# Softmax attention on pairs of heads, with the position bias reversed ahead of it, and a later slot for one subtraction after each norm

## The chip, the cores and the metric

The kernel runs on one core of a Trainium2 chip. Its time is the device time of one execution in microseconds (us). The core has TensorE (PE; its weight loads are listed as PEld), VectorE (DVE), ScalarE (ACT), GpSimd (POOL) and SyncE (SP), which issues DMAs. TensorE writes its results to PSUM, eight banks of 128 x 512 fp32; everything else works from SBUF. Each engine executes its instructions in the order in which they are written, and waits on semaphores for the others.

## The reference

The program is a stack of three blocks on 512 tokens of width 1024, all in fp32: two layers of `first_block`, then `second_block`. Each layer of the first has two gated feed-forwards, a mixer and a gated projection, with a norm after each; the mixer joins a gated delta rule, a stick-breaking attention and this one:

```python
def mla_attention(q_nope, q_rope, k_nope, k_rope, v):      # 4 heads, 96 values of q and k, 64 of v
    s = (einsum(qn, k_nope) + einsum(qr, k_rope)) * scale
    s = where(kpos <= qpos, s, -inf)                       # causal
    pr = softmax(s); return einsum(pr, v)
```

The mixer of the second block joins a sparse attention and a linear recurrence:

```python
def dsa_attention(q, k, v, q_idx, k_idx, w_idx, rel_bias): # 8 heads of 64
    score = sum over index heads of relu(q_idx . k_idx) * w_idx
    top_idx = top_k(score, 128)                            # the keys a query may see
    logits = q . k * HEAD_DIM ** -0.5 + rel_bias[t5_bucket(key - query)]
    p = softmax(logits over those keys); return p @ v

def rg_lru_branch(xr, gate, ...):
    r, i = sigmoid(xg @ w_a + b_a), sigmoid(xg @ w_i + b_i)
    a = exp(-8 * r * softplus(-lam)); b = sqrt(1 - a * a) * i * xc
    h = associative_scan(a, b); return h * gelu(gate)
```

## The kernel before

Activations stand transposed, features on partitions and the 512 tokens (`S`) along the row; a chunk is 128 features by 512 tokens. Weights come in blocks of 128 output features. Each block is loaded by SP, rounded by ScalarE (L171) and its remainder taken by VectorE (L178), and each product is three matmuls of rounded parts (L192 to L194). The program is a chain of stages; at the end of each all engines meet (`stage`, L121). The order on each engine is the order of the code.

`attention` (L1894) serves both softmax attentions. A unit is one head h and one block t of 128 queries, of w = (t + 1) * 128 keys, so the four units of a head have 128, 256, 384 and 512 columns. For a unit TensorE computes scores into one of four PSUM banks, VectorE masks them into SBUF (L2013 and L2014 in the first attention, L2429 in the second) and takes the maximum (L2015, L2430) and its negative (L1966), ScalarE takes exponentials with their sum (L1989), VectorE inverts the sum (L1952), GpSimd multiplies (L2000), TensorE transposes the weights block by block three units later (L1921), and VectorE copies them to SBUF (L1958). When the four units of a head are in, `weigh` (L1930) multiplies them with the values, four matmuls of 512, 384, 256 and 128 columns. ScalarE takes out each pair of heads (L1983). In the trace the first attention is `mix_ma`, the second `b_att`, the heads' outputs `heads_out`.

The bias of the second attention depends on key minus query. A DMA (L2457), in the stage `recurrence` before it (`b_rec`), lays out each head's row with a shift of one per partition, which gives it with the queries upside down; for every unit a matmul with the constant `flip` turns it over and adds it to the scores (L2424), ahead of the product of queries and keys (L2425). An fp32 matmul shows as two records of PE, a transpose as one. A head's queries and keys take 64 partitions, even heads the lower half, odd heads the upper.

In `recurrence` ScalarE evaluates two sigmoids, then per chunk two exponentials and a hyperbolic tangent (L2483 to L2485), then the roots (L2488), which need another table; VectorE then runs per chunk a product, a scan and the product with the gate (L2513 to L2515).

`NormHalves` ends each norm of the first block inside the stage that follows. VectorE multiplies x with the inverse deviation (L318) and subtracts the shift (L323), for parts of 1, 1, 2, 2 and 2 chunks; ScalarE applies gain and bias (L302) and rounds (L305); VectorE takes the remainder, `low` (L311), in the places that the loop at L315 gives. `multiply_first` lets TensorE begin with the chunks that are ready. The stages are the mixer's projections (`mix_proj`), the second feed-forward (`ffb`) and the gated projection (`ple`), each in two layers.

Of the kernel before, what the change touches and what calls it, by code (L numbers as in the profile page):

```python
# [20 lines left out]
F32 = mybir.dt.float32  # L21
# [6 lines left out]
P = 128  # L28
# [251 lines left out]
class NormHalves:  # L280
# [27 lines left out]
    def vector(self, dve, x_high, x_low, beside=nothing):  # L308
# [7 lines left out]
        for part, (begin, end) in enumerate(self.PARTS):  # L316
# [7 lines left out]
            if part > 0:  # L324
                low(n_low)
                n_low += 1
# [1564 lines left out]
RING = 4  # L1891


def attention(nc, name, heads, scores, masked, values, out, scale, const, preload=False):  # L1894
# [5 lines left out]
    units = [(h, t) for h in range(heads) for t in range(NT)]  # L1900
    dims = 64
    with ExitStack() as ctx:
        sb = lambda n, s: ctx.enter_context(nc.sbuf_tensor(f"{name}_{n}", s, F32))
        bank = lambda n: ctx.enter_context(nc.psum_tensor(f"{name}_{n}", [P, S], F32))
        sc, p, pt = sb("sc", [P, 2, S]), sb("p", [P, RING, S]), sb("pt", [P, 2, NT, S])
        stat = sb("stat", [P, RING, 4])
        ps, pr, po = ([bank(f"{n}{j}") for j in range(k)] for n, k in (("s", RING), ("t", 2), ("o", 2)))
        with stage(nc, name, ["scored", "dve_step", "max_ready", "exp_ready", "inverted", "normed", "turned",
                              "pt_ready", "o_done", "o_taken"]) as (
                block, scored, dve_step, max_ready, exp_ready, inverted, normed, turned,  # L1910
                pt_ready, o_done, o_taken):

            @block.tensor
            def _(pe):
                def turn(n):

                    h, t = units[n]
                    pe.wait_ge(normed, n + 1)
                    at_least(pe, pt_ready, n - 1)
                    for s in range(t + 1):  # L1920
                        mm = pe.transpose(pr[n % 2][:, s * P:(s + 1) * P], p[:, n % RING, s * P:(s + 1) * P], const["ident"])  # L1921
                    mm.then_inc(turned, 1)

                def weigh(h):
                    rows = slice(h % 2 * dims, (h % 2 + 1) * dims)
                    pe.wait_ge(pt_ready, NT * (h + 1))
                    if h % 2 == 0:
                        at_least(pe, o_taken, h // 2 - 1)
                    for s in range(NT):
                        mm = pe.matmul(po[h // 2 % 2][rows, s * P:], values(h, s), pt[:, h % 2, s, s * P:],  # L1930
                                       start=s == 0, stop=s == NT - 1, skip_group_check=True)
# [900 lines left out]
```

## Time and profile before

| | us |
|---|---|
| three runs, median (lowest to highest) | 3978.52 (3978.36 to 3985.76) |
| the profiled execution, its own time | 3990.3 |
| its span in the profile | 3988.5 |
| TensorE busy in the span | 3628.1 |
| mean granted clock of TensorE | 0.95 of full speed |

The rows below are lines of one profiled execution. Times are us from the start of the span unless marked ns. A line of a timeline has its start, its length, the engine, the source line, the operation, output<-inputs, the shape, and in brackets the idle time before it and who ended it. A line of windows has the stretch and its length, then busy us with the number of instructions for PE, PEld, DVE, ACT and POOL, then the granted clock of TensorE (1.00 is 2.4 GHz, 0.50 is 1.2 GHz), the share of DMA and GB/s. The end of a matmul is modelled and matmuls overlap, so the distance between starts is its cost. The profile shortens `b2_` to `b_`.

### The profile page before, as it was taken

How to read it: one execution, taken by the hardware profiler on the slowest of the kernel's cores; microseconds unless marked ns; L12 is line 12 of the kernel's file. 1: busy time of each engine (PE TensorE's matmuls, PEld its weight loads, DVE VectorE, ACT ScalarE, POOL GpSimd, SP SyncE). 2: the span in 40 equal slices, each digit the busy share in tenths (PEclk: the TensorE clock that was granted, in tenths of full speed). 3: DMA queues.
4: the chain of work that ended last, by engine and by line, in shares of the span. 5: the costliest groups of instructions: out<-in, count | busy, mean ns of one | idle time of the engine just before them, and what ended most of it. 6: DMA issues, size and time to landing. Idle time of an engine off the chain costs nothing. (4 is left out here: it accounts for less than half of the span.)

```text
span 3988.5 us, 47143 instructions
## 1 busy us (share of the span) xinstructions
PE 3628.1 (91%) x19474; PEld 2768.7 (69%) x19474; DVE 1779.6 (45%) x2352; ACT 1198.9 (30%) x1683; POOL 520.2 (13%) x466
## 2 busy tenths in 40 slices
PE   7999897898999799989979899987999797869997
PEld 5888664676887578867638577865888575347886
DVE  5542365445642455333555455333332365643322
ACT  2222333233222322233332422224222324223221
POOL 0002012430002000020134200021000200330001
PEclk9999999899999899999989899998999898879998
DMA  4432110013331233312100133312333122012231
GB/s 153 142 120 87 63 59 28 2 44 111 135 119 64 90 132 138 107 62 74 65 1 4 59 136 137 105 59 70 93 94 107 52 79 69 1 53 82 94 106 58
DMA packets 88133, 324.23 MB, mean 81 GB/s; under 512 B 12648, under 2 KB 14696, under 8 KB 87536
## 3 DMA queue, kind: packets, MB, share of 16 engines
q1 hardware_dynamic: 87920, 321.21, 24.0%
q8 instruction: 155, 2.54, 0.3%
q14 instruction: 58, 0.48, 0.0%
HBM read 319.06 MB, written 2.12 MB: 81 GB/s over the span
## 5 line engine op out<-in xcount | busy, mean ns | idle before, releaser
L178 DVE TENSOR_TENSOR w_low<-w_raw,w_high 128x1024 fp32r<-128x1024 f32 (+2 forms) x496 | 636.8, 1285 | 1269.8 <-ACT w_high L171 1269.0
L171 ACT ACTIVATE w_high<-w_raw 128x1024 fp32r<-128x1024 f32 (+2 forms) x496 | 544.7, 1099 | 1436.9 <-PE ffa_ps L194 455.5
L192 PE MATMUL ffa_ps<-ffa_x_high,w_high 128*128 128x512 f32 x704 | 283.1, 402 | 34.9 <-DVE ffa_x_low L238 31.3
L192 PE MATMUL ffb_ps<-ffb_x_high,w_high 128*128 128x512 f32 x704 | 285.6, 406 | 27.4 <-DVE ffb_x_low L311 21.4
L192 PE MATMUL b_f_ps<-b_f_x_high,w_high 128*128 128x512 f32 x704 | 281.6, 400 | 18.7 <-DVE b_f_x_low L359 15.1
L193 PE MATMUL ffb_ps<-ffb_x_low,w_high 128*128 128x512 f32 x704 | 283.0, 402 | 0.0
L193 PE MATMUL ffa_ps<-ffa_x_low,w_high 128*128 128x512 f32 x704 | 281.5, 400 | 0.0
L194 PE MATMUL ffb_ps<-ffb_x_high,w_low 128*128 128x512 f32 x704 | 281.4, 400 | 0.0
L194 PE MATMUL ffa_ps<-ffa_x_high,w_low 128*128 128x512 f32 x704 | 281.1, 399 | 0.0
L193 PE MATMUL b_f_ps<-b_f_x_low,w_high 128*128 128x512 f32 x704 | 280.3, 398 | 0.0
L194 PE MATMUL b_f_ps<-b_f_x_high,w_low 128*128 128x512 f32 x704 | 280.1, 398 | 0.0
L192 PE MATMUL mix_proj_ps<-mix_x_high,w_high 128*128 128x512 f32 x432 | 178.4, 413 | 25.8 <-DVE mix_x_low L311 22.4
L192 PEld LDWEIGHTS ffa_ps<-ffa_x_high,w_high 128*128 128x128 f32 x704 | 134.1, 190 | 67.4 <-DVE w_low L178 36.1
L192 PEld LDWEIGHTS ffb_ps<-ffb_x_high,w_high 128*128 128x128 f32 x704 | 134.5, 191 | 66.6 <-issue 24.0
L192 PEld LDWEIGHTS b_f_ps<-b_f_x_high,w_high 128*128 128x128 f32 x704 | 134.1, 190 | 56.1 <-issue 16.9
L193 PE MATMUL mix_proj_ps<-mix_x_low,w_high 128*128 128x512 f32 x432 | 172.3, 399 | 0.0
L194 PE MATMUL mix_proj_ps<-mix_x_high,w_low 128*128 128x512 f32 x432 | 172.2, 398 | 0.0
L194 PEld LDWEIGHTS ffb_ps<-ffb_x_high,w_low 128*128 128x128 f32 x704 | 134.5, 191 | 32.0
L194 PEld LDWEIGHTS b_f_ps<-b_f_x_high,w_low 128*128 128x128 f32 x704 | 134.2, 191 | 31.7
L194 PEld LDWEIGHTS ffa_ps<-ffa_x_high,w_low 128*128 128x128 f32 x704 | 133.9, 190 | 31.6
L193 PEld LDWEIGHTS ffa_ps<-ffa_x_low,w_high 128*128 128x128 f32 x704 | 134.0, 190 | 31.4
L193 PEld LDWEIGHTS ffb_ps<-ffb_x_low,w_high 128*128 128x128 f32 x704 | 134.7, 191 | 30.2
(519 smaller groups left out, 6863.2 us busy)
## 6 DMA issues: line engine op xcount, KB each, us to landing
w_raw<-in_ffa_in SPq DMA_DIRECT2D x88, 512.0 KB, 3.3
w_raw<-in_ffb_in SPq DMA_DIRECT2D x88, 512.0 KB, 3.3
w_raw<-in_ffn_in SPq DMA_DIRECT2D x88, 512.0 KB, 3.5
w_raw<-in_mix_in SPq DMA_DIRECT2D x80, 512.0 KB, 3.4
w_raw<-in_ffa_out SPq DMA_DIRECT2D x32, 704.0 KB, 4.0
w_raw<-in_ffb_out SPq DMA_DIRECT2D x32, 704.0 KB, 4.0
w_raw<-in_ffn_out SPq DMA_DIRECT2D x32, 704.0 KB, 4.0
ffa_ada_raw<-in_w_ada SPq DMA_DIRECT2D x36, 512.0 KB, 4.2
```

The costliest lines, as they stand in the source:

```text
L171: act.activation(self.high[:, n % HALVES, :cols], self.raw[:, n % SLOTS, :cols], ACT.Copy).then_inc(self.rounded, 1)
L178: dve.tensor_tensor(self.low[:, n % HALVES, :cols], self.raw[:, n % SLOTS, :cols], self.high[:, n % HALVES, :cols].bitcast(F32), ALU.subtr ...
L192: pe.matmul(out, w_high, x_high[:, k0 + k, :], start=start and k == 0, stop=False)
L193: pe.matmul(out, w_high, x_low[:, k0 + k, :], start=False, stop=False)
L194: mm = pe.matmul(out, w_low, x_high[:, k0 + k, :], start=False, stop=stop and k == kt - 1)
```

## The change

A unit becomes a pair of heads g and one block t of queries; the buffers have a third index a for the head of the pair. There are two score tiles of two banks each, two banks `pr` for transposes (one for each head of the pair) and two for outputs. TensorE scores both heads of unit n when the exponentials of unit n - 2 are done, transposes unit n - 3 and weighs unit n - 4 block by block, with matmuls of 128 columns that alternate between the two heads. VectorE masks, reduces and scales for both heads in one instruction each; in the first attention the mask is added in place in PSUM, to the last 128 columns alone, and ScalarE reads the scores from PSUM. ScalarE copies the transposed weights in place of VectorE. GpSimd's multiplication is a tensor_tensor over both heads with the inverse repeated. In the second attention GpSimd also adds bias and selection mask into `added`, one unit ahead, and VectorE adds that to the scores. The bias is turned over in `recurrence`, by eight matmuls of 512 columns after the gates and eight copies on ScalarE after the tanh of the last chunk. In `NormHalves` the second `low` of a part is taken only for a chunk of an earlier part.

```diff
-            if part > 0:
+            if n_low < begin:
                 low(n_low)
                 n_low += 1
...
-                for n, (h, t) in enumerate(units):
-                    at_least(pe, max_ready, n - RING + 1)
-                    scores(pe, h, t, ps[n % RING]).then_inc(scored, 1)
-                    if n >= RING - 1:
-                        turn(n - RING + 1)
-                    if t == NT - 1 and h:
-                        weigh(h - 1)
...
+                def turn(n):
+                    g, t = units[n]
+                    pe.wait_ge(normed, n + 1)
+                    for a in range(2):
+                        at_least(pe, pt_ready, 2 * (n - 1) + a + 1)
+                        for s in range(t + 1):
+                            mm = pe.transpose(pr[a][:, s * P:(s + 1) * P], p[:, n % ring, a, s * P:(s + 1) * P], const["ident"])
+                        mm.then_inc(turned, 1)
+                def weigh(n):
+                    g, t = units[n]
+                    pe.wait_ge(pt_ready, 2 * (n + 1))
...
+                    for s in range(t + 1):
+                        for a in range(2):
+                            mm = pe.matmul(po[g % 2][a * dims:(a + 1) * dims, t * P:(t + 1) * P], values(2 * g + a, s),
+                                           pt[:, n % 2, a, s * P:(s + 1) * P], start=s == 0, stop=s == t, skip_group_check=True)
+                for n in range(count + ring):
+                    if n < count:
+                        at_least(pe, exp_ready, 2 * (n - 1))
+                        for a in range(2):
+                            mm = scores(pe, *units[n], a, ps[n % 2])
+                        mm.then_inc(scored, 1)
+                    if 0 <= n - ring + 1 < count:
+                        turn(n - ring + 1)
+                    if n >= ring:
+                        weigh(n - ring)
...
+                        source = masked(dve, own, units[n][1], ps[n % 2], p[:, slot, :, :], added and added[:, n % 2, :, 0:w])
+                        own(dve.tensor_reduce(top[:, slot, :], source, AX_X, ALU.max))
+                        dve.tensor_scalar(shift[:, slot, :], top[:, slot, :], -scale, None, ALU.mult).then_inc(max_ready, 1)
+                    if n:
+                        dve.wait_ge(exp_ready, 2 * n)
+                        dve.reciprocal(inverse[:, (n - 1) % ring, :], total[:, (n - 1) % ring, :]).then_inc(inverted, 1)
...
+                        for a in range(2):
+                            source = p[:, slot, a, 0:w] if bias else ps[n % 2][:, a, 0:w]
+                            act.activation(p[:, slot, a, 0:w], source, ACT.Exp, bias=shift[:, slot, a:a + 1], scale=scale,
+                                           accum_out=total[:, slot, a:a + 1]).then_inc(exp_ready, 1)
+                    if n >= ring - 1:
+                        take(n - ring + 1)
...
+                    if bias and n + 1 < count:
+                        add(n + 1)
+                    pool.wait_ge(inverted, n + 1)
+                    pool.tensor_tensor(p[:, slot, :, 0:w], p[:, slot, :, 0:w], repeat(inverse[:, slot, :], 2, w), ALU.mult)\
                         .then_inc(normed, 1)
...
 def sparse_attention(nc, name, m, const):
-        pe.matmul(ps[:, 0:w], const["flip"], m.bias[:, h, S - w:S], start=True, stop=False)
-        return pe.matmul(ps[:, 0:w], m.q[rows, h // 2, t * P:w], m.k[rows, h // 2, 0:w], start=False, stop=True)
+        return pe.matmul(ps[:, a, 0:w], m.q[rows, g, t * P:w], m.k[rows, g, 0:w], start=True, stop=True)
+    def bias(pool, dst, g, t):
+        return pool.tensor_tensor(dst, m.bias[:, 2 * g:2 * g + 2, S - w:S], repeat(m.drop[:, t, 0:w], 1, 2), ALU.add)
+        own(dve.tensor_tensor(p[:, :, 0:w], ps[:, :, 0:w], added, ALU.add))
...
 def recurrence(nc, name, m, rows_dram, const):
+                pe.wait_ge(bias_landed, 16)
+                for h in range(AH):
+                    at_least(pe, bias_ready, h - 3)
+                    pe.matmul(flipped[h % 4][:, :], const["flip"], m.bias[:, h, :], start=True, stop=True).then_inc(bias_flipped, 1)
...
+                for h in range(AH):
+                    act.wait_ge(bias_flipped, h + 1)
+                    act.activation(m.bias[:, h, :], flipped[h % 4][:, :], ACT.Copy).then_inc(bias_ready, 1)
                 for c in range(LC):
                     act.wait_ge(variance, c + 1)
                     act.activation(a2[:, c, :], a2[:, c, :], ACT.Sqrt).then_inc(rooted, 1)
```

TensorE in the second attention before, from the second head's third block on (`b_att_s` scores, `b_att_t` transposed weights, `b_att_o` outputs, `squares` the constants):

```order
L2424 MATMUL b_att_s<-b_bias,squares 128x384
L2425 MATMUL b_att_s<-b_k,b_q 128x384
L1921 MATMUL b_att_t<-squares,b_att_p 128x128 x4
L2424 MATMUL b_att_s<-b_bias,squares 128x512
L2425 MATMUL b_att_s<-b_k,b_q 128x512
L1921 MATMUL b_att_t<-squares,b_att_p 128x128
L1930 MATMUL b_att_o<-b_att_pt,b_v 64x512
L1930 MATMUL b_att_o<-b_att_pt,b_v 64x384
L1930 MATMUL b_att_o<-b_att_pt,b_v 64x256
L1930 MATMUL b_att_o<-b_att_pt,b_v 64x128
```

The same engine and stage now, from the second pair's first block on:

```order
L2431 MATMUL b_att_s<-b_k,b_q 128x128 x2
L1922 MATMUL b_att_t<-squares,b_att_p 128x128 x4
L1932 MATMUL b_att_o<-b_att_pt,b_v 64x128 x2
L2431 MATMUL b_att_s<-b_k,b_q 128x256 x2
L1922 MATMUL b_att_t<-squares,b_att_p 128x128 x6
L1932 MATMUL b_att_o<-b_att_pt,b_v 64x128 x4
L2431 MATMUL b_att_s<-b_k,b_q 128x384 x2
L1922 MATMUL b_att_t<-squares,b_att_p 128x128 x8
L1932 MATMUL b_att_o<-b_att_pt,b_v 64x128 x6
```

The matmul with `flip` is gone, and each unit now ends with weighing in pieces of 128 columns.

ScalarE in the recurrence before, its last chunk (`b_rec_a`, `b_rec_th` the exponentials and the tanh):

```order
L2483 ACTIVATE b_rec_a<-b_rec_r,b_rec_slope 128x512
L2484 ACTIVATE b_rec_a<-b_rec_r,b_rec_twice 128x512
L2485 ACTIVATE b_rec_th<-b_rec_r,b_rec_minus 128x512
L2488 ACT_TABLE_LOAD
L2488 ACTIVATE b_rec_a<-b_rec_a 128x512 x4
```

And now (`b_rec_flip` the turned bias):

```order
L2497 ACTIVATE b_rec_a<-b_rec_r,b_rec_slope 128x512
L2498 ACTIVATE b_rec_a<-b_rec_r,b_rec_twice 128x512
L2499 ACTIVATE b_rec_th<-b_rec_r,b_rec_minus 128x512
L2502 ACTIVATE b_bias<-b_rec_flip 128x512 x8
L2505 ACT_TABLE_LOAD
L2505 ACTIVATE b_rec_a<-b_rec_a 128x512 x4
```

Eight copies stand between the last tanh and the roots' table load.

VectorE after the norm ahead of the mixer before, from the third part on:

```order
L318 TENSOR_TENSOR state<-state,norm 128x1024
L311 TENSOR_TENSOR mix_x_low<-state,mix_x_high 128x512
L323 TENSOR_TENSOR state<-state,norm 128x1024
L311 TENSOR_TENSOR mix_x_low<-state,mix_x_high 128x512
L318 TENSOR_TENSOR state<-state,norm 128x1024
L311 TENSOR_TENSOR mix_x_low<-state,mix_x_high 128x512
L323 TENSOR_TENSOR state<-state,norm 128x1024
L311 TENSOR_TENSOR mix_x_low<-state,mix_x_high 128x512
```

And now:

```order
L318 TENSOR_TENSOR state<-state,norm 128x1024
L311 TENSOR_TENSOR mix_x_low<-state,mix_x_high 128x512
L323 TENSOR_TENSOR state<-state,norm 128x1024
L318 TENSOR_TENSOR state<-state,norm 128x1024
L311 TENSOR_TENSOR mix_x_low<-state,mix_x_high 128x512
L323 TENSOR_TENSOR state<-state,norm 128x1024
L311 TENSOR_TENSOR mix_x_low<-state,mix_x_high 128x512
```

The next part's product now stands ahead of the `low` that waits for the part just finished.

## Rows read from the trace of the kernel before

**Rows 1.** The page, part 1: busy us, share of the span, instructions

```profile
PE 3628.1 (91%) x19474; PEld 2768.7 (69%) x19474; DVE 1779.6 (45%) x2352; ACT 1198.9 (30%) x1683; POOL 520.2 (13%) x466
```

**Rows 2.** Windows: first attention twice, recurrence, second attention; columns in the text above

```profile
656.80:694.30 37.50, 27.44 (x104) 14.26 (x104) 27.10 (x92) 11.55 (x34) 17.25 (x16) 0.91 0.00 1
2017.60:2055.90 38.30, 29.27 (x104) 15.30 (x104) 27.25 (x92) 11.54 (x34) 17.25 (x16) 0.87 0.00 1
3368.30:3400.60 32.30, 8.80 (x16) 3.54 (x16) 13.65 (x22) 21.42 (x31) 4.98 (x4) 0.62 0.20 65
3400.60:3490.70 90.10, 87.40 (x272) 39.43 (x272) 52.67 (x160) 24.26 (x69) 34.59 (x32) 0.85 0.00 1
```

**Rows 3.** Timeline of PE, second attention, clock full: start, duration, engine, line, tiles

```profile
3432.55 0.66 PE L1921 MATMUL b_att_t<-squares,b_att_p 128*128 128x128 f32 x4
...
3433.04 1.02 PE L2424 MATMUL b_att_s<-b_bias,squares 128*128 128x512 f32 x2
...
3433.99 1.12 PE L2425 MATMUL b_att_s<-b_k,b_q 64*128 64x512 f32 x2
...
3435.05 0.33 PE L1921 MATMUL b_att_t<-squares,b_att_p 128*128 128x128 f32 x1
...
3435.30 2.37 PE L1930 MATMUL b_att_o<-b_att_pt,b_v 128*64 128x512 f32 x8
```

**Rows 4.** Timeline of PE, first attention in layer 0: its first four scores

```profile
656.79 2.40 PE L2007 MATMUL mix_ma_s<-mix_km,mix_qm 96*128 96x128 f32 x8 [2.18 <-PEq L128]
```

**Rows 5.** Timeline of PE: key selection, 64-row matmuls in alternating halves

```profile
3290.68 3.42 PE L2255 MATMUL b_proj_keys_ps<-b_ki,b_qi 64*128 64x512 f32 x10
```

**Rows 6.** Groups of the second attention: count, busy us, mean ns, idle before

```profile
L1989 ACT ACTIVATE b_att_p<-b_att_sc,b_att_stat 128x128 f32<-128x128 f32 (+3 forms) x32 | 18.0, 562 | 59.8 <-DVE b_att_stat L1966 59.6
...
L2429 DVE TENSOR_TENSOR b_att_sc<-b_att_s,b_drop 128x128 f32<-128x128 f32 (+3 forms) x32 | 15.7, 491 | 30.7 <-PE b_att_s L2425 28.5 <-POOL b_att_p L2000 2.2
...
L1989 ACT ACTIVATION_READ_ACCUMULATOR b_att_p<-b_att_sc,b_att_stat 128x1 f32 x32 | 6.0, 186 | 0.0
...
L1983 ACT ACTIVATE b_heads_out<-b_att_o 128x512 f32<-128x512 f32 x4 | 2.3, 582 | 6.0 <-PE b_att_o L1930 6.0
```

**Rows 7.** Groups of GpSimd by shape, whole span

```profile
L1553 POOL TENSOR_TENSOR mix_gc_nb<-mix_gc_lt,squares 128x512 f32<-128x512 f32 x48 | 60.5, 1272 | 81.1 <-PE mix_gc_py L1366 50.1 <-DVE mix_gc_xt L1612 31.0
...
L604 POOL TENSOR_TENSOR ffa_sq_sum<-ffa_sq_sum,ffa_square 128x512 f32<-128x512 f32 x10 | 18.4, 1839 | 22.2 <-ACT ffa_square L618 21.9
...
L905 POOL TENSOR_TENSOR gdn<-gdn,squares 128x128 f32<-128x128 f32 x32 | 15.5, 483 | 5.6 <-ACT gdn L886 5.6
```

**Rows 8.** Windows: clock in the second attention's start, then in the first

```profile
3400.60:3424.00 23.40, 23.36 (x42) 9.70 (x42) 9.45 (x31) 5.70 (x15) 5.83 (x6) 0.50 0.00 1
...
3427.00:3430.00 3.00, 3.00 (x15) 1.70 (x13) 0.67 (x4) 0.00 (x0) 0.27 (x1) 0.91 0.00 0
664.00:668.00 4.00, 4.00 (x11) 2.60 (x12) 3.19 (x12) 0.85 (x3) 2.13 (x3) 0.50 0.00 0
```

**Rows 9.** Timeline of the recurrence: table load before the roots, first root's user

```profile
3386.77 1.28 ACT L2488 ACT_TABLE_LOAD   x1
...
3388.73 0.69 DVE L2513 TENSOR_TENSOR b_rec_th<-b_rec_a,b_rec_i 128x512 f32<-128x512 f32 x1 [1.25 <-ACT b_rec_a L2488]
```

**Rows 10.** Timelines: waits for x_low after norms, mix and ffb, both layers

```profile
433.68 0.47 PE L192 MATMUL mix_proj_ps<-mix_x_high,w_high 128*128 128x512 f32 x1 [1.28 <-DVE mix_x_low L311]
...
926.06 0.48 PE L192 MATMUL ffb_ps<-ffb_x_high,w_high 128*128 128x512 f32 x1 [1.68 <-DVE ffb_x_low L311]
...
1789.28 0.47 PE L192 MATMUL mix_proj_ps<-mix_x_high,w_high 128*128 128x512 f32 x1 [0.73 <-DVE mix_x_low L311]
...
1794.39 0.47 PE L192 MATMUL mix_proj_ps<-mix_x_high,w_high 128*128 128x512 f32 x1 [1.73 <-DVE mix_x_low L311]
...
1793.55 0.69 DVE L311 TENSOR_TENSOR mix_x_low<-state,mix_x_high 128x512 fp32r<-128x512 f32 x1 [1.54 <-ACT mix_x_high L305]
...
2288.57 0.48 PE L192 MATMUL ffb_ps<-ffb_x_high,w_high 128*128 128x512 f32 x1 [0.42 <-DVE ffb_x_low L311]
```

More of the change, by code:

```diff
@@ L1888, in _, with attention @@
                     turn(h + 1, m.qm[rope, h, :])
[L1891 to L1901, printed above, removed]
+def attention(nc, name, pairs, scores, masked, values, out, scale, const, preload=False, bias=None):
+    units = [(g, t) for g in range(pairs) for t in range(NT)]
+    dims, ring = 64, 4
     with ExitStack() as ctx:
[L1903 to L1908, printed above, removed]
+        sb = lambda n, *s: ctx.enter_context(nc.sbuf_tensor(f"{name}_{n}", [P, *s], F32))
+        bank = lambda n, *s: ctx.enter_context(nc.psum_tensor(f"{name}_{n}", [P, *s], F32))
+        p, pt = sb("p", ring, 2, S), sb("pt", 2, 2, S)
+        added = sb("added", 2, 2, S) if bias else None
+        top, shift, total, inverse = (sb(n, ring, 2) for n in ("top", "shift", "total", "inverse"))
+        ps = [bank(f"s{j}", 2, S) for j in range(2)]
+        pr, po = [bank(f"t{j}", S) for j in range(2)], [bank(f"o{j}", S) for j in range(2)]
+        with stage(nc, name, ["scored", "dve_step", "bias_ready", "max_ready", "exp_ready", "inverted", "normed", "turned",
                               "pt_ready", "o_done", "o_taken"]) as (
-                block, scored, dve_step, max_ready, exp_ready, inverted, normed, turned,
+                block, scored, dve_step, bias_ready, max_ready, exp_ready, inverted, normed, turned,
                 pt_ready, o_done, o_taken):
+            count = len(units)
             @block.tensor
@@ L1993, in _, with take, take_out @@
-                take_out(heads // 2 - 1)
+                def take(n):
+                    w = (units[n][1] + 1) * P
+                    for a in range(2):
+                        act.wait_ge(turned, 2 * n + a + 1)
+                        at_least(act, o_done, n - 1)
+                        act.activation(pt[:, n % 2, a, 0:w], pr[a][:, 0:w], ACT.Copy).then_inc(pt_ready, 1)
+                def take_out(g):
+                    act.wait_ge(o_done, NT * (g + 1))
+                    act.activation(out(g), po[g % 2][:, :], ACT.Copy).then_inc(o_taken, 1)
@@ L2009, in masked, with scores @@
[L2009 to L2018 removed]
+    def scores(pe, g, t, a, ps):
+        h, w = 2 * g + a, (t + 1) * P
+        return pe.matmul(ps[:, a, 0:w], m.qm[0:MQ, h, t * P:w], m.km[0:MQ, h, 0:w], start=True, stop=True)
@@ L2021, in first_mixer, with masked @@
+    def masked(dve, own, t, ps, p, added):
+        last = ps[:, :, t * P:(t + 1) * P]
+        own(dve.tensor_tensor(last, last, repeat(const["causal"], 1, 2), ALU.add))
+        return ps[:, :, 0:(t + 1) * P]
+    attention(nc, name, MH // 2, scores, masked, lambda h, s: m.vm[:, s, h * MV:(h + 1) * MV],
+              lambda g: m.o[:, GC + SBH // 2 + g, :], float(MQ) ** -0.5, const)
 def first_mixer(nc, ws, name, halves, m, const, dram):
```

115 lines of the change are left out of this document (40 added, 75 removed).

## Prediction, made before the changed kernel was run

> **What bounds the kernel now.** First the page: TensorE is busy for 3628 of 3988 us [rows 1], so only a place where it stalls, or works more than the output needs, can give time. Then one row of windows for each touched stage [rows 2]: the first attention takes 37.5 us in layer 0 and 38.3 in layer 1, the recurrence 32.3, the second attention 90.1. Within them TensorE is busy for 27.4, 29.3, 8.8 and 87.4. So the second attention is bound by TensorE, the first by the hand-over between engines, and the recurrence by ScalarE and then VectorE, with TensorE out of work. The clock comes next [rows 8]: for the first 23.4 us of the second attention it is 0.50 though TensorE is never idle, and it is back (0.91) only in 3427 to 3430; the first attention has such a spell too, at 664. The last view is the timeline around the norms' ends [rows 10].
>
> All terms below are against the profiled execution (3990.3 us, span 3988.5); the forecast moves the median of the three runs, 3978.5, by the same amount.
>
> **Prices.** At full clock, per pass: a score of 512 columns costs 0.95 us with 128 rows and 1.06 with 64 (3433.04 to 3433.99 to 3435.05) [rows 3], and four transposes 0.49, thus 0.12 each. A head's weighing is 2.37 us, of which some 0.17 is the tail of the last matmul. The four scores of a head with 96 rows are 2.40, or 2.23 without the tail [rows 4]. At half clock I double all of these.
>
> **Second attention.** (a) The bias's matmuls leave the stage: 0.95 us for 512 columns (3433.04 to 3433.99 [rows 3]), 1280 columns a head thus 2.4, eight heads 19 us at full clock, more in the part at half clock. (b) The scores of a pair now follow each other in alternating halves of the partitions. The trace has that form: ten records of 512 columns in 3.42 us [rows 5], 0.33 each against 0.53 for the lone one of rows 3. With 320 columns on average and four records, a unit costs 0.83 us; without overlap it is 1.32, the other bound. (c) On average a unit has five transposes (20 for a pair's four units): five by 0.12 is 0.6, I take 0.57. (d) Weighing in pieces of 128 columns: the multiplications are the same columns, two heads' 2.2 without the tail, 4.4 us a pair, so 1.1 a unit; the weight loads rise from 8 to 20 records a head and hide as those of the transposes do. If the two column halves overlap as the rows do, it is 0.55. I take 1.1. TensorE then needs 2.5 us a unit, 40 for sixteen.
>
> (e) VectorE: an instruction for 320 columns takes 0.49 [rows 6], for two heads 0.83 (twice, less one fixed part of 0.15). Addition, maximum and the small scaling come to 1.9. (f) ScalarE: two exponentials and their reads 1.4, two copies 0.85 (0.58 for 512 columns, less for fewer). (g) GpSimd: 0.48 us for 128 columns and 1.27 for 512 [rows 7] make 2.1 ns a column, so 0.74, 1.28, 1.81 and 2.34 for the four sizes of a pair, 6.2 for all; bias and normalising both need it, 12.3 a pair, 49 for the stage. The dearest row is 1.84 for 512 [rows 7], which makes 18.3 a pair and 73 for the stage. I take the first, the commonest (48 instructions).
>
> (h) The loop: with two score tiles, unit n's scores wait for the exponentials of n - 2, and stand on TensorE behind the transposes and weighing of iteration n - 1, which wait for ScalarE's copies of iteration n - 2. So two units need at least 2.5 + 1.9 + 1.4 + 0.85 and about 0.3 for five hand-overs, 6.95 us: 3.5 a unit, above TensorE's 2.5 and GpSimd's 3.1. Sixteen units make 56. At the end come the last unit's normalising 2.3, transposes 0.9, copies 1.1, weighing 0.9, output 0.6; the first three units have nothing to transpose or weigh, which gives 3 back: 59. (i) The clock: at half clock TensorE's part of two units' round is 2.5 us longer, which makes 4.7 instead of 3.5 a unit; a spell of 26 us as now would cost 6.6. I take nearly all of it, 6: **65, from 90.1: -25**.
>
> In the Trainium skill, "TensorEngine Tiling (Array Packing)", section "Key Properties", says that different tiles of the array can run at the same time, but also that changing the tiling mode drains TensorE. The trace agrees with the first half (0.33 against 0.53 a record). The second speaks against this change, which goes from half rows to the whole array to half columns in every unit; rows 3 put a change at about 0.1 us (1.06 less 0.95), so 48 changes would be 5 us in the stage if each lay in the loop. By that the stage would be 68.
>
> The Trainium skill, "GPSIMD Engine Reference", section "Specifications", puts GpSimd's contention with VectorE at instructions of VectorE with two SBUF inputs. Here VectorE's additions have one input in PSUM. By that rule GpSimd keeps the 1.27 [rows 7] and needs 49 us; by the row of 1.84 it is 73. No row of before has this pair of operations side by side.
>
> **First attention, twice.** TensorE: a pair has the scores of two heads, 2 x 2.23 over its four units, 1.12 a unit; with transposes 0.57 and weighing 1.1 it is 2.8. VectorE's mask is now 256 columns (0.42), the maximum 0.83: 1.5 with the scaling. ScalarE 1.4 + 0.85, hand-overs 0.3. Two units take 6.85, one 3.4, eight 27.4. With the end (5.8) and 2.5 back at the start it is 31. A half-clock spell of 7 us, as at 664, costs 2. So 33 against 37.5 and 38.3: **-9.8** together. Bounds: 29.5 with no spell (-17), and 46 with the clock at half throughout, where TensorE's 5.6 a unit is the bound (+16).
>
> **Recurrence.** TensorE's first four turned heads are ready before ScalarE ends the last tanh at 3386.8 and cost nothing; the cover is that TensorE is idle there. ScalarE makes four copies at 0.5, which frees banks one by one; TensorE, by then at half clock, needs 1.75 us (0.95 doubled, less a fixed part) for each of the last four from 3387.4 on, so the last copy ends near 3395. Only then come table load and first root: the product that waits for it, now at 3388.7 [rows 9], moves by **+8.2** (3395 less 3386.8). All of VectorE's chain behind it moves with it. Bounds: 4.9 with TensorE at full clock, 9 with later starts. The DMA of the bias (issued with the stage's start) has landed by then.
>
> **Norms' ends.** VectorE now does the next part's product (1024 columns, by the 0.69 of 512 some 1.25) in the 1.54 us for which it waits for ScalarE [rows 10]. From the fourth part on each `low` comes earlier, the last by about 3.3. The last waits of TensorE for it are 1.28, 1.68, 0.73 and 1.73, and 0.42 in layer 1's feed-forward [rows 10]: 5.8 us, all gone. In `ple` TensorE waits for weights that stand behind `low` on VectorE; I take 1 us for each layer, between 0 and 3.3. **-7.8**. What is late next is the third block's remainder, which waits for TensorE itself.
>
> **Sum.** -25 - 9.8 + 8.2 - 7.8 = -34.4: 3944 us.
>
> **The rivals.**
> - *GpSimd becomes the bound.* For it: with 3.1 us a unit it has more work than TensorE's 2.5 even at the lower price, and a row of 1.84 [rows 7] is the higher. Against: 48 instructions show the lower price, 10 the higher. The stage is 73 + 8 = 81, a gain of 9: the sum is -18.4, 3960.
> - *More overlap.* Column halves overlap too and the clock holds. The second attention is 57 and the first 29.5 each: -33 - 17 + 5 - 8 = -53, 3926. For it: rows 5. Against: the clock fell in both stages.
> - *Half clock for half of each stage.* The short 128-column work leaves TensorE waiting in the loop, 2.5 of 3.5 us busy. Attentions at 76 and 40 each: -14 + 4 = -10, and the rest cancels: 3969.
> - *Slower: half clock to the end in both attentions.* Then TensorE needs 5.0 to 5.6 us a unit and binds: 86 to 102 us in the second, 46 twice in the first (+16). With 86 that is -4 + 16 + 0.4 = +12, 3991; with 102 it is +28. It decides from the point where TensorE is slow for more than about two thirds of both stages. For it: rows 8, 23 us at 0.50 with TensorE never idle. Against: once up, the clock stayed up through the rest of both stages with TensorE 73% busy or less [rows 2], and it will be 71 to 82% busy.
> - *The change does not do what it says:* the bias's matmuls could return as waits. They are not in the stage any more, so only the clock and GpSimd can take the gain back; both are above.
>
> **How the numbers follow.** Forecast 57% (own range 3932 to 3956), more overlap 10%, GpSimd 15%, half clock for half of it 10%, slower 8%. The range to hold 8 of 10 is 3924 to 3968. A measurement can tell 0.2%, 8 us, from no change, not less. Faster by more than that: the first three and half of the fourth, 87%; within it 6%; slower 7%.
>
> **What would show it.** The second attention's window near 65 us with TensorE some 65% busy, and pairs of 512-column scores starting within 1.4 us; eight units of the first near 33; the first root's user near 20 us (now 20.4) + 8 from the recurrence's start; no wait of TensorE for `x_low` after its fourth chunk. GpSimd idle for under a tenth of the second attention would mean the first rival, a clock below 0.75 over the stages the third or fourth. The forecast is wrong if either attention's loop is longer than 4.2 us a unit, or if the recurrence grows by over 10.

## The result, and the profile after

The changed kernel takes 3956.15 us (median of four runs, 3955.25 to 3957.4) against 3982.14 (3978.36 to 3986.51) for the kernel before: a ratio of 0.9932, 95% interval 0.9918 to 0.9945, or 26 us less. Forecast were 34 less and 3944. The 3956 lies in the stated range, but 26 less is about as near to the rival in which GpSimd becomes the bound (18 less) as to the forecast, so the whole time alone does not choose between them. The profiled executions differ by 34 (spans 3988.5 and 3954.6), but that of before was 8 us over its median, so their agreement with the sum of the terms is an accident. The terms must be read one by one.

The page of the changed kernel, part 1, beside [rows 1]:

```profile
PE 3586.2 (91%) x19618; PEld 2761.9 (70%) x19618; DVE 1729.2 (44%) x2136; ACT 1221.4 (31%) x1755; POOL 515.1 (13%) x450
```

The touched stages, from barrier to barrier, in the order first attention twice, recurrence, second attention. First the kernel before (the windows of [rows 2], drawn out to the barriers), then the changed one:

```profile
656.60:695.20 38.60, 27.45 (x104) 14.30 (x104) 27.10 (x92) 11.55 (x34) 17.25 (x16) 0.91 0.00 1
2017.50:2056.40 38.90, 29.27 (x104) 15.30 (x104) 27.25 (x92) 11.54 (x34) 17.25 (x16) 0.87 0.00 1
...
3400.50:3492.30 91.80, 87.40 (x272) 39.43 (x272) 52.67 (x160) 24.26 (x69) 34.59 (x32) 0.85 0.00 1
```

```profile
652.50:687.70 35.20, 28.09 (x152) 18.09 (x152) 12.50 (x32) 15.97 (x50) 10.02 (x8) 0.76 0.01 1
2001.00:2036.00 35.00, 28.24 (x152) 18.27 (x152) 12.50 (x32) 15.97 (x50) 10.03 (x8) 0.76 0.00 1
3335.30:3375.30 40.00, 18.93 (x32) 7.56 (x32) 13.65 (x22) 25.73 (x39) 5.00 (x4) 0.69 0.15 53
3375.30:3460.80 85.50, 53.66 (x304) 32.22 (x304) 30.20 (x64) 33.39 (x101) 43.97 (x32) 0.65 0.00 1
```

The second attention's engines have far less to do (TensorE 53.7 us in place of 87.4), no engine is busy for more than 63% of it, and yet it is only 6.3 us shorter. That is where the expected gain went. Its timeline shows why. One steady stretch of the changed kernel, picked rows of GpSimd and VectorE:

```profile
3423.79 1.04 POOL L2011 TENSOR_TENSOR b_att_p<-b_att_p,b_att_inverse 128x512 f32<-128x512 f32 x1 [2.49 <-DVE b_att_inverse L1964]
...
3424.79 2.34 POOL L2435 TENSOR_TENSOR b_att_added<-b_bias,b_drop 128x1024 f32<-128x1024 f32 x1
...
3427.33 1.23 DVE L2439 TENSOR_TENSOR b_att_p<-b_att_s,b_att_added 128x1024 f32<-128x1024 f32 x1 [3.62 <-POOL b_att_added L2435]
...
3428.59 1.22 DVE L1960 TENSOR_REDUCE b_att_top<-b_att_p 128x2 f32<-128x1024 f32 x1
3429.85 0.17 DVE L1961 TENSOR_SCALAR b_att_shift<-b_att_top 128x2 f32<-128x2 f32 x1
3429.92 0.16 DVE L1964 RECIPROCAL b_att_inverse<-b_att_total 128x2 f32<-128x2 f32 x1
...
3430.16 1.47 POOL L2011 TENSOR_TENSOR b_att_p<-b_att_p,b_att_inverse 128x768 f32<-128x768 f32 x1 [3.03 <-DVE b_att_inverse L1964]
```

Read it as a ring, which is a closed loop of waits. GpSimd normalises unit n, then adds bias and mask for n + 2; VectorE waits for just that (3.62 us), then adds, reduces and scales n + 2, and only behind that inverts the sum of n + 1; GpSimd waits for just that (3.03) and normalises n + 1. The two take turns. A pair of heads, four units, takes 19.9 us (3418.91 to 3438.81). GpSimd's eight instructions (0.61, 1.81, 1.04, 2.34, 1.47, 0.72, 1.89, 1.26) are 11.1 of it, its four waits for the inverse (2.49, 3.03, 1.43, 1.96) the other 8.9. That is 4.98 a unit, 80 for the stage, and more than the 4.2 a unit that the prediction named as a sign of being wrong.

The groups of the same stage name it too, in their last column (the 29.2 ahead of the first is one wait, for the stage to begin):

```profile
L2435 POOL TENSOR_TENSOR b_att_added<-b_bias,b_drop 128x256 f32<-128x256 f32 (+3 forms) x16 | 24.5, 1535 | 29.2 <-SPq L125 29.2
L2011 POOL TENSOR_TENSOR b_att_p<-b_att_p,b_att_inverse 128x256 f32<-128x256 f32 (+3 forms) x16 | 20.0, 1252 | 34.2 <-DVE b_att_inverse L1964 34.2
...
L2439 DVE TENSOR_TENSOR b_att_p<-b_att_s,b_att_added 128x256 f32<-128x256 f32 (+3 forms) x16 | 13.2, 825 | 44.8 <-POOL b_att_added L2435 37.1 <-PE b_att_t L1922 5.3 <-PE b_att_s L2431 2.3
```

In the recurrence the table load ahead of the roots and the first root's user answer to [rows 9]:

```profile
3361.69 1.28 ACT L2505 ACT_TABLE_LOAD   x1
...
3363.64 0.69 DVE L2530 TENSOR_TENSOR b_rec_th<-b_rec_a,b_rec_i 128x512 f32<-128x512 f32 x1 [9.12 <-ACT b_rec_a L2505]
```

From the stage's start that user stands at 28.3 us, against 20.4. Of the waits for `x_low` in [rows 10] none is left in mix or ffb. The last one in layer 0's mixer is now this, for the third chunk, and the other three stages have one of the same length at the same place:

```profile
421.07 0.79 PE L192 MATMUL mix_proj_ps<-mix_x_high,w_high 128*128 128x512 f32 x1 [1.72 <-DVE mix_x_low L311]
```

### The profile page after: what moved, and what is told of

It reads as the page before. It is cut to its first block and busy times, and to the rows that moved or that the text cites. A ratio compares the mean times of both kernels' runs of the same rounds, so it can differ in the third digit from the quotient of the medians.

```text
span 3954.6 us, 47146 instructions
## 1 busy us (share of the span) xinstructions
PE 3586.2 (91%) x19618; PEld 2761.9 (70%) x19618; DVE 1729.2 (44%) x2136; ACT 1221.4 (31%) x1755; POOL 515.1 (13%) x450
## 5 line engine op out<-in xcount | busy, mean ns | idle before, releaser
L192 PE MATMUL ffa_ps<-ffa_x_high,w_high 128*128 128x512 f32 x704 | 281.7, 400 | 35.4 <-DVE ffa_x_low L238 31.8
L193 PEld LDWEIGHTS b_f_ps<-b_f_x_low,w_high 128*128 128x128 f32 x704 | 133.8, 190 | 30.7
L193 PEld LDWEIGHTS ffb_ps<-ffb_x_low,w_high 128*128 128x128 f32 x704 | 133.7, 190 | 30.6
```

The costliest lines, as they stand in the source:

```text
L192: pe.matmul(out, w_high, x_high[:, k0 + k, :], start=start and k == 0, stop=False)
L193: pe.matmul(out, w_high, x_low[:, k0 + k, :], start=False, stop=False)
```

## The experiments

The ratios are to the kernel before, run on the same chip between the others, with 95% intervals. Stages are from barrier to barrier in one profiled execution each. The same code differs there from run to run: the recurrence of the changed kernel has 40.1 us here and 38.5 in add_two_ahead, the first attention of before 38.6 and 38.9 here and 37.9 and 37.4 in norms_only.

| | ratio | first attention | recurrence | second attention |
|---|---|---|---|---|
| before | 1 | 38.6, 38.9 | 32.2 | 91.8 |
| norms_only | 0.9963 (0.9951 to 0.9976) | 37.9, 37.4 | 32.2 | 91.8 |
| changed kernel | 0.9932 (0.9918 to 0.9945) | 35.3, 35.0 | 40.1 | 85.5 |
| add_two_ahead | 0.9867 (0.9851 to 0.9884) | 35.2, 35.0 | 38.5 | 62.2 |
| inverse_first | 0.9906 (0.9889 to 0.9922) | 35.1, 35.0 | 38.9 | 74.5 |
| warm | 0.9941 (0.9927 to 0.9955) | 31.8, 35.0 | 40.1 | 85.5 |
| take_first | 0.9932 (0.9917 to 0.9947) | 29.8, 29.2 | 40.1 | 84.7 |
| roots_first | 0.9906 (0.9883 to 0.9928) | 35.1, 34.9 | 32.2 | 86.0 |
| by_head | one run, 3958.5 us | 32.6, 35.7 | 40.1 | 85.7 |
| add2_roots_take | 0.9834 (0.9816 to 0.9851) | 29.2, 30.6 | 32.2 | 57.2 |
| scale_on_act | 0.9821 (0.9805 to 0.9838) | 29.7, 30.6 | 32.2 | 55.2 |
| warm_start | 0.9835 (0.9817 to 0.9854) | 30.8, 29.4 | 32.2 | 57.3 |
| no_addition | one run, 3913.2 us | 27.1, 29.2 | 32.2 | 53.9 |

**norms_only.** The kernel before with the `NormHalves` part of the diff alone.

> The kernel before with one part of the change alone: after a norm the second low of a part is taken only for a chunk of an earlier part. The prediction's price is -7.8 us for all six places (5.8 in mix and ffb, 1 in each ple). In the profile of the changed kernel the stages mix_proj are 1.6 and 1.5 us shorter, ffb 3.2 and 6.6, ple 5.7 and 3.0, in all 21.6, part of it the clock (ffb of layer 1 has 0.4 us to win at its wait). Theory (waits alone): -6 to -10 us, a ratio of 0.9975 to 0.9985. Rival (the norms' ends bring most of the whole kernel's gain): -20 us, 0.995. Other rival (the gain is in the profile only): 0, 1.000.

Its stages give -1.6 and -1.6 us in mix_proj, -3.3 and -2.6 in ffb, -5.4 and -2.6 in ple: -17.1. The ratio gives -14.7 (-9.6 to -19.5). That is between the first theory and the rival, and about twice the forecast of 7.8. By the medians this part brings more than half of what the whole change does; the interval allows from a third to three quarters. Layer 0's ple, the kernel before and then this one:

```profile
1321.86 0.69 DVE L311 TENSOR_TENSOR ple_x_low<-state,ple_x_high 128x512 fp32r<-128x512 f32 x1 [1.54 <-ACT ple_x_high L305]
1322.94 0.51 PE L192 MATMUL ple_proj<-ple_p_high,w_high 128*128 128x512 f32 x1 [2.04 <-DVE w_low L178]
1325.82 0.50 PE L192 MATMUL ple_ps<-ple_x_high,w_high 128*128 128x512 f32 x1 [1.21 <-DVE w_low L178]
```

```profile
1314.76 0.69 DVE L311 TENSOR_TENSOR ple_x_low<-state,ple_x_high 128x512 fp32r<-128x512 f32 x1
1315.84 0.50 PE L192 MATMUL ple_proj<-ple_p_high,w_high 128*128 128x512 f32 x1 [0.41 <-DVE w_low L178]
1318.71 0.50 PE L192 MATMUL ple_ps<-ple_x_high,w_high 128*128 128x512 f32 x1 [1.21 <-DVE w_low L178]
```

VectorE's wait ahead of the `low` is gone, and TensorE's wait for the weights behind it is 0.41 in place of 2.04. The first gate product starts 20.1 us after the barrier (1298.6) in place of 21.7 (1304.1), which is 1.6 of the 5.4. TensorE's clock over the stage is 0.93 in place of 0.89, and other runs of the same ple code in layer 0 took from 74.7 us at 0.93 to 78.2 at 0.90. So about 3 us of the 5.4 come and go with the clock. The same holds elsewhere: layer 1's ffb, 3 us shorter here, took from 394 to 398 us in runs of the same code.

**add_two_ahead.** The changed kernel with

```diff
                 if bias:
                     add(0)
+                    add(1)
                 for n in range(count):
-                    if bias and n + 1 < count:
-                        add(n + 1)
+                    if bias and n + 2 < count:
+                        add(n + 2)
```

> The changed kernel, with GpSimd's addition of bias and mask issued two units ahead in place of one, so that the addition of unit n + 2 stands ahead of the normalising of unit n on GpSimd. Theory (a ring of GpSimd and VectorE bounds the second attention: normalising of n, addition of n + 2, VectorE's add, maximum, scaling of n + 2, inverse of n + 1, normalising of n + 1; 1.25 + 1.54 + 0.83 + 0.82 + 0.17 + 0.16 and hand-overs make 4.9 us a unit, 78 of the 85.5): the ring is cut, VectorE does not wait for the addition, the stage falls to 58 to 66 us (3.2 to 3.6 a unit) and the whole by 20 to 27 against the changed kernel, about 3933, ratio 0.987 to 0.989. Rival (TensorE at 1.2 GHz bounds the stage): the stage stays at 83 to 86 and the ratio at 0.993. Rival (GpSimd's durations bound it): the stage is above 80 with GpSimd idle for under a tenth.

62.2 us, from 85.5, and the whole 0.9867: the theory, with a ratio just under the 0.987 that it named. GpSimd has the same 32 instructions of the same length, TensorE's clock is 0.50 in the first 15.6 us here as there, and neither of the rivals can give the 23 us. GpSimd in this kernel, over one pair:

```profile
3405.11 0.61 POOL L2012 TENSOR_TENSOR b_att_p<-b_att_p,b_att_inverse 128x256 f32<-128x256 f32 x1 [0.17 <-DVE b_att_inverse L1964]
3405.68 2.37 POOL L2436 TENSOR_TENSOR b_att_added<-b_bias,b_drop 128x1024 f32<-128x1024 f32 x1
3408.76 1.04 POOL L2012 TENSOR_TENSOR b_att_p<-b_att_p,b_att_inverse 128x512 f32<-128x512 f32 x1 [0.71 <-DVE b_att_inverse L1964]
3409.75 0.72 POOL L2436 TENSOR_TENSOR b_att_added<-b_bias,b_drop 128x256 f32<-128x256 f32 x1
...
3418.89 0.61 POOL L2012 TENSOR_TENSOR b_att_p<-b_att_p,b_att_inverse 128x256 f32<-128x256 f32 x1 [0.17 <-DVE b_att_inverse L1964]
```

A pair takes 13.78 us, 3.45 a unit, where the prediction had 3.5 for its loop of scores, VectorE, exponentials and copies.

**inverse_first.** The ring cut at its other joint, GpSimd's order as in the changed kernel:

```diff
                 for n in range(count + 1):
+                    if n and bias:
+                        dve.wait_ge(exp_ready, 2 * n)
+                        dve.reciprocal(inverse[:, (n - 1) % ring, :], total[:, (n - 1) % ring, :]).then_inc(inverted, 1)
                     slot = n % ring
...
-                    if n:
+                    if n and not bias:
```

> The changed kernel, with one order of VectorE altered in the second attention alone: the inverse of unit n - 1 is taken ahead of the masking of unit n in place of behind its maximum. GpSimd's order stays, its addition still one unit ahead. Theory (a ring of GpSimd and VectorE bounds the stage): this cuts the ring at its other joint; GpSimd's normalising of n and addition of n + 2 (2.8 us) then run beside VectorE's and ScalarE's work on unit n + 1 (0.83 + 0.82 + 0.17 + first and second exponentials 1.4 + 0.2 = 3.4, and hand-overs), so 3.6 to 3.9 us a unit and a stage of 65 to 71 in place of 85.5; whole 15 to 20 us under the changed kernel, ratio 0.988 to 0.990. Rival (only GpSimd's order matters, the additions come too late whatever VectorE does): 84 to 87.

74.5 us: the stage gets 11 shorter, so the rival falls, but it is 3.5 over the theory's bound, and the ratio of 0.9906 is at the weak end too. VectorE's wait for the addition is gone, and another has come, as its row (the mask's addition) and ScalarE's show:

```profile
L1992 ACT ACTIVATE b_att_p<-b_att_p,b_att_shift 128x128 f32<-128x128 f32 (+3 forms) x32 | 17.7, 553 | 36.0 <-DVE b_att_shift L1964 36.0
...
L2442 DVE TENSOR_TENSOR b_att_p<-b_att_s,b_att_added 128x256 f32<-128x256 f32 (+3 forms) x16 | 13.2, 825 | 4.6 <-PE b_att_s L2434 3.7 <-POOL b_att_added L2438 0.9
```

VectorE now stands at the inverse until the second exponential is read, then masks, reduces and scales for the next unit, and ScalarE waits for that: a ring of VectorE and ScalarE, 16.4 us a pair (3409.31 to 3425.67), 4.1 a unit. In it VectorE's small scaling, 0.17 us in the changed kernel, has a mean of 0.75: 11 of the 16 last until a running instruction of GpSimd ends, as here.

```profile
3409.55 1.89 POOL L2014 TENSOR_TENSOR b_att_p<-b_att_p,b_att_inverse 128x1024 f32<-128x1024 f32 x1 [2.29 <-DVE b_att_inverse L1953]
...
3410.40 1.07 DVE L1964 TENSOR_SCALAR b_att_shift<-b_att_top 128x2 f32<-128x2 f32 x1
```

That is 9.3 us more in the stage (12.0 in place of 2.8), on VectorE's side of the ring, and enough to explain the miss of 3.5, though no run parts it from the rest.

**warm.** The changed kernel with, behind the turned heads on TensorE,

```diff
+                for k in range(11):
+                    pe.matmul(ps[k % 4][:, :], const["flip"], m.xc[:, 0, :], start=True, stop=True)
```

> The changed kernel with eleven matmuls of 512 columns more on TensorE in the recurrence, behind the turning over of the bias, into banks that nobody reads; they run beside VectorE's scans, so TensorE comes into the second attention out of work instead of out of idleness. Theory (the ring of GpSimd and VectorE): whatever the clock then does at its start, the second attention stays within 2 us of 85.5. Rival (the clock bounds it): with the clock at full speed at the start the stage falls by 5 to 15 us. The recurrence itself should stay at 40 us.

85.5 us again. But the clock at the second attention's start was 0.50 all the same, after 5 us without work behind the last of the eleven, so the run doesn't tell the ring from the clock. It showed something else: layer 0's first attention, whose code it does not touch, took 31.8 us at a mean clock of 0.89, against 35.2 at 0.76.

**take_first.** ScalarE's copies ahead of the exponentials:

```diff
                 for n in range(count + ring - 1):
+                    if n >= ring - 1:
+                        take(n - ring + 1)
                     if n < count:
...
-                    if n >= ring - 1:
-                        take(n - ring + 1)
```

> The changed kernel, with ScalarE's two copies of transposed weights of unit n - 3 ahead of the exponentials of unit n in place of behind them. Theory for the first attention (its loop over two units holds scores, VectorE's part, exponentials and, through TensorE's order, the copies): the copies leave the loop and the stages fall from 35.3 and 35.0 us to 30 to 32 each. In the second attention, which the ring of GpSimd and VectorE bounds, nothing: 84 to 86. Rival (TensorE's own work at its low clock bounds the first attention): 34 to 35 as now. Rival for the second (the hand-over by ScalarE bounds it): 75 to 80. Whole: -6 to -10 us against the changed kernel by the theory.

29.8 and 29.2 us in the first attention (35.3 and 35.0), 84.7 in the second, as the theory had it stage by stage. But 6 to 10 us less were expected for the whole, and it didn't move (0.9932): this profile has 1.7 to 3.5 us more in each of layer 0's mix_proj and ple, layer 1's first gated feed-forward and ple, whose code is the same. The gain of each stage has two parts, which can be told apart only roughly. With the old order at a clock of 0.89 (warm) it is 31.8, with the new one at 0.89 and 0.88 29.8 and 29.2: some 2.3 us go with the order, the other 3.3 with the clock. The clock in turn goes with the order: of the twelve first attentions of this table that have the changed kernel's order, ten are at 0.76, and of the ten with the copies ahead none is under 0.83.

**roots_first.** The eight copies of the turned bias behind the four roots.

```diff
-                for h in range(AH):
-                    act.wait_ge(bias_flipped, h + 1)
-                    act.activation(m.bias[:, h, :], flipped[h % 4][:, :], ACT.Copy).then_inc(bias_ready, 1)
                 for c in range(LC):
                     act.wait_ge(variance, c + 1)
                     act.activation(a2[:, c, :], a2[:, c, :], ACT.Sqrt).then_inc(rooted, 1)
+                for h in range(AH):
...
```

> The changed kernel with the eight copies of the turned bias behind the roots on ScalarE, the rest as it is. The prediction's term for the copies ahead of the roots is +8.2 us; the recurrence has 40.0 us against 32.2 before. Theory (the copies delay the roots' table load and VectorE's chain with it): the recurrence is 32.3 +- 0.5, VectorE's scans cover copies and turning; whole -7.8 against the changed kernel, ratio 0.991. Rival (the copies only change places with the roots and the stage then ends with them): 36 to 40.

The recurrence is 32.2 us, as before: the whole price of turning the bias was its place. The ratio of 0.9906 agrees.

**add2_roots_take.** The edits of add_two_ahead, take_first and roots_first, together.

> The changed kernel with three orders altered: GpSimd's addition two units ahead, ScalarE's copies of transposed weights ahead of the exponentials, and in the recurrence the eight copies of the turned bias behind the four roots. From the stages of the runs so far: second attention 62 or less, first attention 29.5 twice (35.3 and 35.0 in the changed kernel), recurrence back at 32.3 (40.0 there). Theory (the three costs are separate): -23 - 11 - 7.8 = -42 us against the changed kernel, a ratio to before of 0.982 to 0.984. Rival (the second attention starts cold and waits for the last turned heads, so that the recurrence's gain is given back): 0.985.

0.9834 and 57.2 us: the ratio is 0.0098 under the changed kernel's, 39 us, where the theory had 42. The rival's loss is not in the second attention, which is 5 us shorter than with add_two_ahead alone; the ratio's interval just reaches the rival's 0.985.

**scale_on_act.** The same, and the scaling of the maxima moved:

```diff
-                        own(dve.tensor_reduce(top[:, slot, :], source, AX_X, ALU.max))
-                        dve.tensor_scalar(shift[:, slot, :], top[:, slot, :], -scale, None, ALU.mult).then_inc(max_ready, 1)
+                        dve.tensor_reduce(top[:, slot, :], source, AX_X, ALU.max).then_inc(max_ready, 1)
...
+                        own(act.activation(shift[:, slot, :], top[:, slot, :], ACT.Copy, scale=-scale))
```

> The version with all three orders altered, and VectorE's small scaling (128x2, 0.17 us alone, but up to 1.50 and 0.45 in the mean beside GpSimd's additions with the addition two units ahead) done by ScalarE ahead of the exponentials. Theory (VectorE's instruction is held up by GpSimd's running one, which costs 0.28 us a unit in the mean): the second attention is 3 to 5 us shorter than without, 57 to 59. Rival (the hold-up is beside the bound, and ScalarE's own step of 0.2 to 0.25 is as long): within 1 us, or 1 longer in each attention.

55.2 from 57.2, between theory and rival, and nothing in the first attention, where GpSimd is busy for 10 us of 30. The ratio of 0.9821 isn't clear of 0.9834, and warm_start, with the same attention code, has 57.3: so a gain in the stage isn't shown. It is the fastest complete version by its median, 3913.3 us.

**no_addition.** Add2_roots_take without GpSimd's addition: VectorE adds the selection mask alone, and the position bias is left out of the result.

> The version with all three orders altered, with GpSimd's addition left out: VectorE adds the selection mask alone to the scores, the position bias is not added at all. GpSimd then has 20 us of work in the second attention in place of 44.5. Theory (with the additions two units ahead the loop of scores, VectorE, exponentials bounds the stage): 57 to 61, only the hold-ups of VectorE go. Rival (GpSimd's 2.8 us a unit still bounds it): 50 or less.

53.9 us, 3 under the theory's 57 to 61 and 4 over the rival's 50. Against the 57.2 of add2_roots_take, 24 us of work taken off GpSimd give 3: its amount of work is not what bounds the stage. The hold-ups of VectorE's scaling are part of the 3 (mean 0.28 us in place of 0.40).

**by_head.** The changed kernel, `weigh` with its two loops exchanged.

```diff
-                    for s in range(t + 1):
-                        for a in range(2):
+                    for a in range(2):
+                        for s in range(t + 1):
```

> The changed kernel, with the products of weights and values of one head after those of the other, in place of alternating between the two column halves. In the changed kernel twelve records of 128 columns take 0.81 us from start to start, 0.068 each, at the full clock. Theory (matmuls in the two column halves overlap): without alternation a record takes about 0.107 to 0.11, as 128 columns of a lone product do; TensorE's weighing grows from 17.5 to 22 to 27 us busy, and the stages stay within 1.5 us of 85.5 and 35 where TensorE isn't the bound. Rival (128-column pieces are cheap for another reason): 0.07 as before.

Twelve records at full clock take 1.08 us from start to start (3423.24 to 3424.32) in place of 0.81 (3421.40 to 3422.21), 0.090 each in place of 0.068. Alternating halves do overlap, but the saving is a quarter, since 0.090 is already under the 0.107 of the theory; the weighing is busy for 19.9 us in the stage, against 17.5 and 22 to 27 expected. The second attention (85.7) and layer 1's first attention (35.7) did not move. Layer 0's took 32.6, more than the 1.5 us allowed off, at a clock of 0.90 in place of 0.76, as in warm.

```profile
3423.24 1.15 PE L1932 MATMUL b_att_o<-b_att_pt,b_v 128*64 128x128 f32 x12
3424.32 1.13 PE L2431 MATMUL b_att_s<-b_k,b_q 64*128 64x512 f32 x4
```

**warm_start.** Scale_on_act with eleven fillers ahead of the fifth turned head and four behind the eighth.

> The version with all orders altered and the scaling on ScalarE (second attention 55.2 us, at 0.50 of the clock for its first 13 to 15), with fifteen more matmuls of 512 columns on TensorE in the recurrence, eleven ahead of the fifth turned head and four behind the eighth, into banks that nobody reads, to keep TensorE at work until the stage ends. Theory (what is left in the second attention is partly the cold start): if the granted clock there starts at 1.00, the stage falls by 3 to 6 us, to 50 to 52, the recurrence stays at 32.2, ratio 0.980 to 0.981. Rival (the loop of scores, VectorE and ScalarE holds it whatever the clock): within 1 us of 55.2. If the clock still starts at 0.50 the run tells nothing of either.

The recurrence, and the second attention's first 5.7 us:

```profile
3338.10:3370.30 32.20, 28.78 (x62) 12.19 (x62) 13.65 (x22) 25.65 (x39) 4.99 (x4) 0.94 0.19 65
3370.30:3376.00 5.70, 3.91 (x14) 1.98 (x16) 3.14 (x6) 3.66 (x11) 5.48 (x5) 0.50 0.01 4
```

TensorE ran the recurrence at 0.94, but over the barrier (2.6 us without work) it fell to 0.50 again. By the expectation's own condition this says nothing of what a warm start would bring, and that stays open. The stage took 57.3 us, 2.1 more than in scale_on_act with the same code, which is the spread that a difference between two profiles has to beat.

## Why the prediction was right, and where it was wrong

**Second attention, -25 forecast, -6.3 measured: the step that failed is (h).** It took the stage's loop to be scores, VectorE, exponentials and ScalarE's copies, 3.5 us a unit, and weighed GpSimd only by its amount (3.1). The orders themselves make a second loop through GpSimd and VectorE, of 4.98 us: the addition of n + 2 is behind the normalising of n, which waits for an inverse that is behind the maximum of n + 1, which waits for the addition of n + 1. Both halves stood in the change's code and could have been priced from the prediction's own durations: per pair 12.3 for GpSimd and 7.6 for VectorE make 19.9. The trace shows 19.9 too, but with 11.1 for GpSimd and the rest for VectorE and hand-overs, so the exact agreement is luck. With that loop cut at either joint the stage falls (62.2, 74.5), and cut at GpSimd's it comes to 3.45 a unit and, with the rest of the sum unchanged, within 3 us of the 65 forecast. The 68 that the prediction gives for changes of the array's shape should have been 70 by its own terms (65 and 5); at 3.45 a unit no run shows such a cost. GpSimd's price was right: 1.25 in the mean for normalising and 1.54 for the addition (6.2 a pair was forecast, 5.0 and 6.1 measured); the higher row of 1.84 for 512 columns did not come.

**The rivals.** None was it. "GpSimd becomes the bound" had the nearest stage (81) but the wrong mechanism: GpSimd was idle for half of the stage, and halving its work gains 3 us once the order is right. "Half clock" had the right sign in the profile (0.65 over the stage, under the 0.75 named), but the low clock is in good part a result: GpSimd's order alone takes it from 0.65 to 0.78 over the stage and the stage down by 23 us, though the first 15.6 us stay at 0.50. What the prediction had against this rival was misread: it says that the clock stayed up with TensorE 73% busy or less, while TensorE was busy for 73 and 76% of the first attentions and 97% of the second [rows 2].

**First attention, -9.8 forecast, -7.3 measured.** Within the stated bounds. Against the 37.9 and 37.4 that the old attention took in norms_only it is -5.0. The clock is the likely difference: 0.76 over the stage, while a spell of 7 us was forecast, and at 0.89 the same code took 31.8. The copies of ScalarE, which the change leaves on the path, are worth some 2.3 more each.

**Recurrence, +8.2 forecast, +7.8 measured.** Right in mechanism and size, and the root's user at 28.3 us is where it was put. Roots_first gives all of it back. The same code took 38.5 and 38.9 in two other runs, so the size is 6.3 to 7.9.

**Norms' ends, -7.8 forecast, -17 by stages and -14.7 by the ratio.** The waits named are gone; the sizes of ple and ffb were off. Ple was given 1 us a layer, and the waits gave 1.6 in layer 0: the weights' remainders stand behind the `low` on VectorE, so its waits of 1.54 went on to TensorE. The rest of -5.4 and -2.6 was no term of the sum and goes along with the clock. Of ffb's -3.3 and -2.6 the waits named are 1.7 and 0.4; the rest is not explained, and is within what the same code differs from run to run.

**Sum.** -6.3 - 7.3 + 7.8 - 17.1 - 1.0 (the merge after the attention) = -24, against -26 measured. Two errors, +19 in the second attention and -9 at the norms' ends, stood against each other. That 3956 lies in the range is in part luck.

## What to carry to other kernels

When work moves to an idle engine, its amount is the smaller question. Write the orders of both engines side by side, follow what each waiting instruction has behind it, and price every closed loop: a loop through two engines costs the sum of its parts though neither is busy for much more than half. Issuing the producer one unit further ahead of the instruction that waits took no further buffer here and was worth 23 us, though the two engines then run side by side and VectorE's scaling is held up by 0.28 us a unit. And an in-order engine's filler work goes behind what others wait for, not ahead of it: eight copies before the roots cost about 8 us, after them none. Last, the same code differed by 2 to 4 us a stage between two profiles, so a smaller gain needs more than one of each.

## What the runs showed of the hardware

A small instruction of VectorE can be held up by GpSimd's running one. In add_two_ahead, VectorE's and GpSimd's rows:

```profile
3399.84 1.26 POOL L2436 TENSOR_TENSOR b_att_added<-b_bias,b_drop 128x512 f32<-128x512 f32 x1
...
3400.04 1.09 DVE L1961 TENSOR_SCALAR b_att_shift<-b_att_top 128x2 f32<-128x2 f32 x1
```

The scaling of 2 columns, 0.17 us when alone, takes 1.09 and ends at 3401.13, as GpSimd's addition does (3401.10). Over the stage its mean is 0.447 against 0.172 in the changed kernel, where the ring keeps the two engines apart. It is 0.75 in inverse_first, behind additions and normalisings alike: the 8 and 11 instances over 0.25 us all end within 0.1 us of GpSimd's instruction. The maxima (0.82) and the inverses (0.16) beside it are not held up, and GpSimd's durations stay the same. The Trainium skill, "GPSIMD Engine Reference", section "Specifications", has VectorE and GpSimd contend where VectorE's instruction is in a 2-port mode or has two SBUF inputs; the prediction took up the second condition alone. The scaling has one input, so by this rule only the first can hold for it. The trace agrees as far as it goes: it shows who is held up, not the mode.
